# Attention scores from three passes over high and low parts of queries and keys, in place of one 32-bit product

## The chip, the cores and the metric

The kernel runs on one NeuronCore of a Trainium2 chip. The metric is the device time of one execution, in microseconds, as the median of several runs; smaller is better. The engines have short names: PE is the matrix engine (TensorE) and PEld its weight loads, ACT is ScalarE, DVE is VectorE, POOL is GpSimd, SP is SyncE, which here issues weight transfers. Each engine works through its own queue in order and waits on semaphores.

## The reference

One layer of a streaming encoder for 1024 prompt frames and 32 sample frames. It has a retention branch, a differential attention branch, a gated convolution network and a per-layer input embedding. The change touches the differential attention alone, whose core is:

```python
def diff_core(q, k, v, mask, lam):
    s = jnp.einsum('bqhmd,bkhmd->bhmqk', q, k, preferred_element_type=jnp.float32) * (DA_DK ** -0.5)
    if mask is not None:
        s = jnp.where(mask, s, jnp.finfo(jnp.float32).min)
    p = jax.nn.softmax(s, axis=-1)
    a = p[:, :, 0] - lam * p[:, :, 1]
    return jnp.einsum('bhqk,bkhe->bqhe', a.astype(v.dtype), v)
```

There are 4 heads with two maps (m = 0, 1) each, and 128 numbers per query and key. The prompt is cut into blocks of 128 queries; a block sees all keys up to its own chunk of 64. The 32 sample queries see 128 cached keys and their own 32. Queries and keys come from a projection of the normed input, are normed and rotated by position.

## The kernel before

**Number formats.** Weights and activations of the large products are kept as a high and a low part (`w_hi`, `w_lo`, `a_hi`, `a_lo`, type float32r), and a product is three PE instructions (`three`, lines 604 to 608: high by high, high by low, low by high). POOL makes the parts of a weight unit of 128x1024 (`split`, lines 497 to 506). A part lies in one of 8 slots; a unit's slot is split again when the last product that reads it is done. The attention scores are instead one plain 32-bit product per block of up to 512 keys (line 830), with the queries `q_t` as weights and the keys `k_t` as the moving operand; the trace records each as two PE instructions.

**Stages.** Gates (up to 200 us), retention (to 490 us), differential attention (490 to 1080 us), then output branches, up and down projections and the embedding.

**Order within differential attention.** All engines walk over the same steps (`for s in range(DIFF_STEPS)`), 12 steps a head. Step s projects token tile s (0 to 7 are prompt tiles of 128 rows, 8 is the 32 sample rows), and works on older tiles with a lag: `turned` is the tile one step back, `scored` two, `weighed` three, `normed` four. The three steps after a head's tiles are `fill` steps, in which PE computes six pieces of two gates from weight slots (`DIFF_GATE_SLOTS`).

PE's order in a step is: first part of the projection to queries and first key map (slots 0 to 2), scores of map 0 of the scored tile, transposes of the weighed tile's attention (line 848), rest of that projection, products with the values (line 857), scores of map 1, projection to second key map and values (slots 4 to 6), transposes of the turned tile's queries and keys into bank 4 (line 995), for tiles with over four blocks the rest of the products with the values, transposes of the normed tile (line 1011).

- Map 0's scores wait for `d_ev` of their tile: two copies on DVE (lines 1948 and 1949), the last DVE work of the step before, which wait for the transposes at line 995.
- Map 1's scores of tiles 4 to 7 wait for map 0's exponential on ACT (line 1426), as both maps use the same banks. Tiles 0 to 3 and 8 (`short`) have a bank for each map.
- ACT's order in a step is: square of the normed tile (line 1354, which waits for the transposes at line 1011 of the step before), squares of the turned tile (line 1370), roots, values (line 1390), normed tile (1399), output rows and their transfer (1411, 1414), then a table load and map 0's exponential (1426), and map 1's (1438).
- DVE's order is: maximum of map 0 (line 1871), in the first fill step the copy of the cached keys (line 1877), the copy of transposed attention that PE's line 857 waits for (line 1885), norms and rotation of the turned tile (1899, 1766 to 1774), maximum of map 1 (1914), weights of the attention (1939), the two copies.
- POOL splits a head's 8 units in this order: three for slots 0 to 2, three for slots 4 to 6, two gates.

Of the kernel before, what the change touches and what calls it, by code (L numbers as in the profile page):

```python
# [22 lines left out]
P = 128  # L23
# [40 lines left out]
EARLY = 3  # L64
PA_SLOT, PB_SLOT = 0, 4
BRIDGE_SLOT = 3
DIFF_GATE_SLOTS = (3, 7)
GATE_BANKS = (3, 2, 0, 1, 3, 2)


# [37 lines left out]
def kernel_program(nc, t):  # L108
    with ExitStack() as ctx:
        def sb(name, shape, dt=F32):  # L110
            return ctx.enter_context(nc.sbuf_tensor(name, shape, dt))
# [15 lines left out]
        a_lo = sb("a_lo", [P, KT * NT], F32R)  # L127

        a_pre = nc.alloc_sbuf_tensor_at("a_pre", [P, KT * NT], F32, offset=a_lo_at)
        full = sb("full", [P, KT * NT])  # L130
        scr = sb("scr", [P, 6 * UW])
        ident = sb("ident", [P, P])
        ones = sb("ones", [P, P])
# [100 lines left out]
        gqk = f.take(2 * P).rearrange("p (g c) -> p g c", g=2)  # L234
        mask = f.take(2 * P)
        k_t_at = f.at
        k_t = f.take(2 * (NT + PAST)).rearrange("p (m n) -> p m n", m=2)
        v_tok = f.take((TILES + 1) * DV).rearrange("p (t c) -> p t c", t=TILES + 1)
        nrm_at = f.at
        nrm = f.take(512)  # L240
        a_t = f.take(1024).rearrange("p (b n) -> p b n", b=8)
        kc = f.take(2 * P)
        rope_b = s.take(512)
        qk = s.take(2 * 512).rearrange("p (b n) -> p b n", b=2)
        e0 = s.take(1024)
        e1 = s.take(1024)
        a_w = s.take(1024)
        q_t = s.take(2 * 2 * P).rearrange("p (b m n) -> p b m n", b=2, m=2)
        o_n = s.take(2 * DV).rearrange("p (b n) -> p b n", b=2)
        o_t = s.take(2 * DV).rearrange("p (b m n) -> p b m n", b=2, m=2)  # L250
        st = s.take(48)


        at = nrm_at + 256
# [66 lines left out]
        def wait_piece(eng, h, n, pieces):  # L321

            eng.wait_ge(pieces, GATE_PIECES + 6 * h + n + 1)
# [55 lines left out]
        def score_bank(m, i):  # L379

            return 5 + m if short(i) else 5
# [114 lines left out]
        def _(pool):  # L496
            def split(before, j, slot, words=8 * P, others=0):


                landed = (before + (j - j % RAW)) * 4 + 16  # L500
                pool.wait_ge(w_landed[j % RAW], landed)
                pool.sem_inc(S["w_begun"], 1)
                raw, hi, lo = w_raw[:, j % RAW, 0:words], w_hi[:, slot, 0:words], w_lo[:, slot, 0:words]
                pool.tensor_scalar(hi, raw, 1.0, 0.0, ALU.mult, ALU.add).then_inc(S["w_hi_done"], 1)  # L504
                pool.wait_ge(S["w_hi_done"], before + (j + 1 - others))
                pool.tensor_tensor(lo, raw, hi.bitcast(F32), ALU.subtract).then_inc(S["w_split"], 1)  # L506
# [17 lines left out]
            for h in range(HEADS):  # L524
                unit = U_DIFF + (8 * h + 1 if h else 0)
                if h:
                    pool.wait_ge(S["pa_done"], h * TILES)
                    pool.wait_ge(S["a_done"], h * TILES - 1)
                else:
                    pool.wait_ge(S["ret_proj"], (HEADS - 1) * TILES)  # L530
                for j in range(3):
                    split(0, unit + j, PA_SLOT + j)
                if h == 0:
                    split(0, U_BRIDGE, BRIDGE_SLOT)
                    unit += 1
                if h:
                    pool.wait_ge(S["pb_done"], h * TILES)
                else:
                    pool.wait_ge(S["ret_proj"], HEADS * TILES)
                for j in range(3):  # L540
                    split(0, unit + 3 + j, PB_SLOT + j)
                for j in range(2):
                    if h:
                        wait_piece(pool, h - 1, 4 + j, S["gate_part"])
                    else:
                        pool.wait_ge(S["acc_done"], A_DIFF)
                    split(0, unit + 6 + j, DIFF_GATE_SLOTS[j])
            for j in range(8):
                if j == 0:
                    pool.wait_ge(S["pa_done"], HEADS * TILES)  # L550
                    pool.wait_ge(S["a_done"], HEADS * TILES - 1)
                if j in DIFF_GATE_SLOTS:
                    wait_piece(pool, HEADS - 1, 4 + (j == DIFF_GATE_SLOTS[1]), S["gate_part"])
                if j == PB_SLOT:
                    pool.wait_ge(S["pb_done"], HEADS * TILES)
                split(U_B, j, j)
            def eight_units(g):
                for j in range(8):
# [44 lines left out]
        def _(pe):  # L603
# [219 lines left out]
            def scores(m, i):  # L823

                keys, first = (P * (i + 1), 0) if i < LAST else (NS + PAST, NP)
                r = rows(i)
                for b in range(0, keys, 512):
                    n = min(512, keys - b)
                    diag = i < LAST and b + n == keys
                    last = pe.matmul(ps[0:r, score_bank(m, i) + b // 512, 0:n], q_t[:, i % 2, m, 0:r],  # L830
                                     k_t[:, m, first + b:first + b + n], start=True, stop=not diag)
                    if diag:
                        last = pe.matmul(ps[0:r, score_bank(m, i) + b // 512, n - P // 2:n], mask[:, 0:P],  # L833
                                         mask[:, P + P // 2:2 * P], start=False, stop=True)
                return last
# [340 lines left out]
        def _(act):  # L1176
# [162 lines left out]
            for s in range(DIFF_STEPS):  # L1339
# [61 lines left out]
                if stored:  # L1401
                    h, i, n = stored
                    r, b = rows(i), i % 2
                    act.wait_ge(S["dot_tr"], n + 1)
                    if n == 0:
                        act.wait_ge(ot_st[0], RET_TILES // 2 * 16)
                        act.wait_ge(ot_st[1], RET_TILES // 2 * 16)
                    if h * (5 - b) + i // 2:
                        act.wait_ge(dot_st[b], (h * (5 - b) + i // 2) * 16)
                    for m in range(2):  # L1410
                        act.activation(o_t[:, b, m, 0:r], ps[:, 7, (2 + m) * P:(2 + m) * P + r], ACT.Copy,
                                       scale=cols[:, 24 + m:25 + m]).then_inc(S["dot_ev"], 1)
                    act.wait_ge(S["dot_ev"], 2 * (n + 1))
                    act.dma_start(o_d[2 * h:2 * h + 2, :, i * P:i * P + r].rearrange("m p n -> p m n"),
                                  o_t[:, b, :, 0:r]).then_inc(dot_st[b], 16)
                if scored:
                    h, i, n = scored
                    r, b = rows(i), i % 2
                    keys = P * (i + 1) if i < LAST else NS + PAST
                    if n == 0:  # L1420
                        act.wait_ge(S["s_out"], HEADS * 32)
                        act.wait_ge(gate_st[0], (FIRST + 3) // 2 * 16)
                    act.wait_ge(S["m0_done"], n + 1)
                    if n >= 1:
                        act.wait_ge(S["a_done"], n)
                    act.activation(e0[0:r, 0:keys], score_rows(0, i), ACT.Exp, bias=st[0:r, 24 + b:25 + b],  # L1426
                                   accum_out=st[0:r, 28 + 2 * b:29 + 2 * b]).then_inc(S["e0_done"], 1)
# [6 lines left out]
                if scored:  # L1434
                    h, i, n = scored
                    r, b = rows(i), i % 2
                    act.wait_ge(S["m1_done"], n + 1)
                    act.activation(e1[0:r, 0:keys], score_rows(1, i), ACT.Exp, bias=st[0:r, 26 + b:27 + b],
                                   accum_out=st[0:r, 29 + 2 * b:30 + 2 * b]).then_inc(S["e1_done"], 1)
                fill = fill_at(s, 1)  # L1440
                if fill:
                    h, k = fill
# [214 lines left out]
        def _(dve):  # L1657
# [191 lines left out]
            for s in range(DIFF_STEPS):  # L1849
# [23 lines left out]
                now = fill_at(s, 0)  # L1873
                if now and now[1] == 0:
                    h = now[0]
                    dve.wait_ge(S["dc_tr"], h + 1)
                    dve.tensor_copy(k_t[:, :, NT:NT + PAST],
                                    ps[:, 2, 0:2 * P].rearrange("p (m n) -> p m n", m=2)).then_inc(S["dc_ev"], 1)
                if weighed:
                    h, i, n = weighed  # L1880
                    r, c = rows(i), min(4, i + 1) if i < LAST else 2
# [59 lines left out]
                if turned:  # L1941
                    h, i, n = turned
                    r, b = rows(i), i % 2
                    dve.wait_ge(S["d_tr"], n + 1)
                    if freed(i, n) > 0:
                        dve.wait_ge(S["s1_done"], freed(i, n))
                    v4 = ps[:, 4, :].rearrange("p (m n) -> p m n", m=4)
                    dve.tensor_copy(q_t[:, b, :, 0:r], v4[:, 0:2, 0:r]).then_inc(S["d_ev"], 1)
                    dve.tensor_copy(k_t[:, :, i * P:i * P + r], v4[:, 2:4, 0:r]).then_inc(S["d_ev"], 1)

            def evict(p):

# [280 lines left out]
```

## Time and profile before

| | us |
|---|---|
| median of 3 runs (lowest, highest) | 2243.19 (2242.13, 2244.16) |
| the profiled execution's own time | 2242.92 |
| its span, first to last instruction | 2241.1 |
| PE busy | 2222.3 (99%) |
| DVE, POOL, ACT busy | 1078.2, 666.0, 654.7 |

The span is what the trace shows; 1.8 us lie around it. A row of the timeline has the start from the span's start and a duration, both in us. PE's durations run past the start of the next instruction, since matmuls are pipelined; the time that one takes in a stream is the distance of the starts.

### The profile page before, as it was taken

What the parts mean: (1) busy time and instruction counts of PE and PEld (TensorE: products, weight loads), DVE (VectorE), ACT (ScalarE), POOL (GpSimd) and SP (SyncE); (2) the same over time, 40 slices, a digit from 0 to 9 for tenths busy, and PEclk for the clock granted to TensorE, in tenths of its full rate; (3) what the DMA queues carried; (4) which work ended last, traced back from release to release, by engine and by line L of the source; (5) the groups of instructions that cost most, each with busy time, mean ns of one, the idle gap of its engine ahead of it and who ended that gap; (6) DMA issues with size and microseconds to landing.
All of it is one profiled execution on the core that took longest, in us unless ns stands there. A gap on an engine that the chain in (4) does not pass through costs nothing.

```text
span 2241.1 us, 34167 instructions
## 1 busy us (share of the span) xinstructions
PE 2222.3 (99%) x13160; PEld 2091.9 (93%) x13160; DVE 1078.2 (48%) x2032; ACT 654.7 (29%) x1519; POOL 666.0 (30%) x368
## 2 busy tenths in 40 slices
PE   8999999999999999999999999999999999999999
PEld 7999777789898898998999999999999999999999
DVE  5312444445535455355145658666666663313432
ACT  5200333335535345354212222110101104334311
POOL 4522210230130400401350534223333325576520
PEclk9999999999999999999999999999999999999999
DMA  7622222230130310302851322222222126656311
GB/s 253 198 92 76 71 69 88 76 103 27 32 108 27 105 40 25 118 27 72 301 169 61 116 64 76 76 67 70 72 66 76 57 68 202 187 162 203 97 50 49
DMA packets 312666, 218.18 MB, mean 97 GB/s; under 512 B 16330, under 2 KB 303677, under 8 KB 312542
## 3 DMA queue, kind: packets, MB, share of 16 engines
q1 hardware_dynamic: 219802, 117.33, 18.1%
q10 hardware_dynamic: 92740, 99.15, 13.1%
q8 instruction: 83, 1.36, 0.3%
q14 instruction: 41, 0.34, 0.0%
HBM read 160.15 MB, written 56.29 MB: 97 GB/s over the span
## 4 chain that ended last, share of the span: by engine, by line
PE 94%; ACT 3%; DMA 1%; issue 1%; DVE 1%; ACTq 1%; DVEq 0%
PE ps L606 28%; PE ps L608 28%; PE ps L607 27%; PE ps L830 3%; PE ps L857 2%; PE ps L780 1%; PE ps L785 1%; PE ps L995 1%; PE ps L782 1%; PE ps L848 1%; ACT L1426 1%; ACT L1377 1%; DMA scr<-inv_d 0%; ACT full L1370 0%; PE ps L833 0%
## 5 line engine op out<-in xcount | busy, mean ns | idle before, releaser
L606 PE MATMUL ps<-a_hi,w_hi 128*128 128x352 f32 x2928 | 950.1, 324 | 5.3 <-DVE a_lo L1674 3.2
L608 PE MATMUL ps<-a_hi,w_lo 128*128 128x352 f32 x2928 | 940.3, 321 | 0.0
L607 PE MATMUL ps<-a_lo,w_hi 128*128 128x352 f32 x2928 | 939.5, 321 | 0.0
L504 POOL TENSOR_SCALAR w_hi<-w_raw 128x1024 fp32r<-128x1024 f32 x150 | 162.9, 1086 | 1435.8 <-PE ps L608 877.5
L606 PEld LDWEIGHTS ps<-a_hi,w_hi 128*128 128x128 f32 x2928 | 549.6, 188 | 9.3 <-issue 8.6
L607 PEld LDWEIGHTS ps<-a_lo,w_hi 128*128 128x128 f32 x2928 | 550.9, 188 | 0.4
L608 PEld LDWEIGHTS ps<-a_hi,w_lo 128*128 128x128 f32 x2928 | 550.4, 188 | 0.0
L506 POOL TENSOR_TENSOR w_lo<-w_raw,w_hi 128x1024 fp32r<-128x1024 f32 x150 | 363.5, 2423 | 12.5
L606 PE MATMUL ps<-w_hi,a_hi 128*128 128x384 f32 (+3 forms) x864 | 318.7, 369 | 0.0
L608 PE MATMUL ps<-w_hi,a_lo 128*128 128x384 f32 (+3 forms) x864 | 307.7, 356 | 0.0
L607 PE MATMUL ps<-w_lo,a_hi 128*128 128x384 f32 (+3 forms) x864 | 306.5, 355 | 0.0
L608 PEld LDWEIGHTS ps<-w_hi,a_lo 128*128 128x128 f32 (+1 forms) x864 | 154.4, 179 | 19.5
L607 PEld LDWEIGHTS ps<-w_lo,a_hi 128*128 128x128 f32 (+1 forms) x864 | 155.5, 180 | 16.8
L606 PEld LDWEIGHTS ps<-w_hi,a_hi 128*128 128x128 f32 (+1 forms) x864 | 154.9, 179 | 16.7
L581 POOL TENSOR_TENSOR w_lo<-w_raw,w_hi 128x1024 fp32r<-128x1024 f32 (+1 forms) x64 | 141.5, 2244 | 74.2 <-ACT w_hi L1571 74.2
L2052 DVE TENSOR_TENSOR scr<-ps,scr 128x704 f32<-128x704 f32 x44 | 39.2, 891 | 131.9 <-PE ps L608 131.9
L1524 ACT ACT_TABLE_LOAD x21 | 26.9, 1283 | 253.0 <-issue 253.0
L2060 DVE COPY u_last<-scr 128x4 f32 (+1 forms) x44 | 88.3, 2006 | 5.7
L1766 DVE TENSOR_TENSOR scr<-ps,full 128x128 f32<-128x128 f32 (+3 forms) x72 | 25.7, 356 | 130.0 <-ACT full L1259 128.8
L2098 DVE TENSOR_TENSOR full<-full,ps 128x352 f32 (+1 forms) x24 | 12.4, 520 | 157.0 <-PE ps L608 157.0
L1259 ACT ACTIVATE full<-ps,u_last 128x256 f32<-128x256 f32 (+1 forms) x36 | 17.0, 472 | 216.2 <-PE ps L608 208.2
L830 PE MATMUL ps<-full,scr 128*128 128x512 f32 (+4 forms) x208 | 77.3, 478 | 1.6 <-ACT scr L1426 1.3
(206 smaller groups left out, 2283.4 us busy)
## 6 DMA issues: line engine op xcount, KB each, us to landing
w_raw<-w_in SPq DMA_DIRECT2D x64, 512.0 KB, 4.2
w_raw<-w_down SPq DMA_DIRECT2D x48, 512.0 KB, 3.6
w_raw<-w_up SPq DMA_DIRECT2D x44, 512.0 KB, 3.7
hid_d<-scr ACTq DMA_DIRECT2D x22, 512.0 KB, 2.6
w_raw<-w_down SPq DMA_DIRECT2D x24, 384.0 KB, 3.2
scr<-gates_d ACTq DMA_DIRECT2D x24, 352.0 KB, 6.1
gates_d<-full ACTq DMA_DIRECT2D x13, 528.0 KB, 2.6
xt_d<-full ACTq DMA_DIRECT2D x1, 4224.0 KB
```

Of the source, the lines that this page charges most:

```text
L504: pool.tensor_scalar(hi, raw, 1.0, 0.0, ALU.mult, ALU.add).then_inc(S["w_hi_done"], 1)
L506: pool.tensor_tensor(lo, raw, hi.bitcast(F32), ALU.subtract).then_inc(S["w_split"], 1)
L581: pool.tensor_tensor(w_lo[:, slot, 0:words], w_raw[:, j % RAW, 0:words], w_hi[:, slot, 0:words].bitcast(F32), ALU.subtract).then_inc(S["w_ ...
L606: pe.matmul(out, lhs[0], rhs[0], start=start, stop=False)
L607: pe.matmul(out, lhs[0], rhs[1], start=False, stop=False)
L608: return pe.matmul(out, lhs[1], rhs[0], start=False, stop=stop)
L830: last = pe.matmul(ps[0:r, score_bank(m, i) + b // 512, 0:n], q_t[:, i % 2, m, 0:r], k_t[:, m, first + b:first + b + n], start=True, stop= ...
L857: last = pe.matmul(ps[0:r, 7, 0:DV], a_t[0:n, b, 0:r], v_tok[0:n, vt, :], start=b == 0, stop=b == every - 1)
L1524: act.activation(row(1, CW), row(1, CW), ACT.Silu).then_inc(S["silu_done"], 1)
L1766: dve.tensor_tensor(bb[:, :, 0, :], x4[:, :, 1, :], sn, ALU.mult).then_inc(prods, 1)
L2052: dve.tensor_tensor(u[:, GAP:GAP + 2 * THIRD].rearrange("p (c n) -> p c n", c=2), src[:, 0:2, :], inv[:, 0:2 * THIRD].rearrange("p (c n) - ...
L2060: dve.tensor_copy(u_last[:, bass.ds(j + half * FT, 1), :].rearrange("p a (s w) -> p (a s) w", w=GAP), ends).then_inc(S["u_last_done"], 1)
```

## The change

Queries and keys of the differential attention get a high and a low part, and each score product becomes `three`. ACT makes the high parts by copies out of PSUM, DVE the low parts by subtraction. The query buffers were two of 32-bit queries (by tile parity) and are now one of high and one of low parts, so ACT's copies wait for the tile before (`s1_done`). The low parts of the prompt keys take slot 7 of the weights (map 0 in `w_hi`, map 1 in `w_lo`); the second gate moves to slot 6, which the values' projection uses as well. The keys of sample and cache have low parts in a buffer of their own (`k_lo_last`, over the raw cached keys).

```diff
-DIFF_GATE_SLOTS = (3, 7)
+DIFF_GATE_SLOTS = (3, 6)
+KEY_SLOT = 7
...
+        k_lo = (w_hi[:, KEY_SLOT, :], w_lo[:, KEY_SLOT, :])
+
+        def key_parts(h, i):
+
+            return TILES + 9 + (TILES + 1) * h + i + 1 + (i == LAST)
...
                 for j in range(3):
+                    if h and PB_SLOT + j == DIFF_GATE_SLOTS[1]:
+                        wait_piece(pool, h - 1, 5, S["gate_part"])
                     split(0, unit + 3 + j, PB_SLOT + j)
                 for j in range(2):
-                    if h:
-                        wait_piece(pool, h - 1, 4 + j, S["gate_part"])
+                    if j:
+                        pool.wait_ge(S["pb_done"], (h + 1) * TILES)
+                    elif h:
+                        wait_piece(pool, h - 1, 4, S["gate_part"])
...
-                    last = pe.matmul(ps[0:r, score_bank(m, i) + b // 512, 0:n], q_t[:, i % 2, m, 0:r],
-                                     k_t[:, m, first + b:first + b + n], start=True, stop=not diag)
+                    high = k_hi[:, m, first + b:first + b + n]
+                    low = k_lo[m][:, b:b + n] if i < LAST else k_lo_last[:, m, :]
+                    last = three(ps[0:r, score_bank(m, i) + b // 512, 0:n], (q_hi[:, m, 0:r], q_lo[:, m, 0:r]),
+                                 (high, low), True, not diag)
...
+                cached = fill_at(s, 0)
+                if cached and cached[1] == 0:
+                    act.wait_ge(S["dc_tr"], cached[0] + 1)
+                    act.activation(k_hi[:, :, NT:NT + PAST], ps[:, 2, 0:2 * P].rearrange("p (m n) -> p m n", m=2),
+                                   ACT.Copy).then_inc(S["xs_done"], 1)
                 if scored:
...
+                if turned:
+                    h, i, n = turned
+                    r = rows(i)
+                    act.wait_ge(S["d_tr"], n + 1)
+                    if n >= 1:
+                        act.wait_ge(S["s1_done"], n)
+                    v4 = ps[:, 4, :].rearrange("p (m n) -> p m n", m=4)
+                    act.activation(q_hi[:, :, 0:r], v4[:, 0:2, 0:r], ACT.Copy)
+                    act.activation(k_hi[:, :, i * P:i * P + r], v4[:, 2:4, 0:r], ACT.Copy).then_inc(S["xs_done"], 1)
...
-                    dve.wait_ge(S["dc_tr"], h + 1)
-                    dve.tensor_copy(k_t[:, :, NT:NT + PAST],
-                                    ps[:, 2, 0:2 * P].rearrange("p (m n) -> p m n", m=2)).then_inc(S["dc_ev"], 1)
+                    dve.wait_ge(S["xs_done"], cache_parts(h))
+                    dve.tensor_tensor(k_lo_last[:, :, NS:NS + PAST], ps[:, 2, 0:2 * P].rearrange("p (m n) -> p m n", m=2),
+                                      k_hi[:, :, NT:NT + PAST].bitcast(F32), ALU.subtract).then_inc(S["dc_ev"], 1)
...
-                    dve.tensor_copy(q_t[:, b, :, 0:r], v4[:, 0:2, 0:r]).then_inc(S["d_ev"], 1)
-                    dve.tensor_copy(k_t[:, :, i * P:i * P + r], v4[:, 2:4, 0:r]).then_inc(S["d_ev"], 1)
+                    dve.tensor_tensor(q_lo[:, :, 0:r], v4[:, 0:2, 0:r], q_hi[:, :, 0:r].bitcast(F32),
+                                      ALU.subtract).then_inc(S["d_ev"], 1)
...
+                        for m in range(2):
+                            last = dve.tensor_tensor(k_lo[m][:, at], v4[:, 2 + m, :], k_hi[:, m, at].bitcast(F32),
+                                                     ALU.subtract)
...
+                    last.then_inc(S["d_ev"], 1)
```

Three places show how the queues change. First ACT, in the first fill step of a head (scored tile 7), from the output rows to the end of the step. Before:

```order
L1411 ACTIVATE scr<-ps,cols 128x128
L1414 DMA o_d<-scr 128x2x128 [waits dot_ev]
L1426 ACT_TABLE_LOAD [waits a_done]
L1426 ACTIVATE scr<-ps,scr 128x1024 [waits m0_done]
L1433 DMA new_k_sample<-scr 32x256 [waits d_rope]
L1438 ACTIVATE scr<-ps,scr 128x1024 [waits m1_done]
L1354 ACTIVATE scr<-ps 128x256 [waits dot_tr,pv_done]
```

Now (the lines are 29 to 34 further down in the changed kernel):

```order
L1440 ACTIVATE scr<-ps,cols 128x128
L1443 DMA o_d<-scr 128x2x128 [waits dot_ev]
L1448 ACTIVATE k_hi<-ps 128x2x128 [waits dc_tr]
L1460 ACT_TABLE_LOAD [waits a_done]
L1460 ACTIVATE scr<-ps,scr 128x1024 [waits m0_done]
L1467 DMA new_k_sample<-scr 32x256 [waits d_rope]
L1472 ACTIVATE scr<-ps,scr 128x1024 [waits m1_done]
L1481 ACTIVATE q_hi<-ps 128x2x32 [waits s1_done,d_tr]
L1482 ACTIVATE k_hi<-ps 128x2x32
L1383 ACTIVATE scr<-ps 128x256 [waits dot_tr,pv_done]
```

The copy of the cached keys stands between the output transfer and the exponential of map 0, and the two copies of the turned tile stand ahead of the next step's first square; in every other step of a turned tile these two are new as well.

Second DVE, at the end of the step of scored tile 6 and the start of that of tile 7. Before:

```order
L1939 SCALAR_TENSOR_TENSOR scr<-scr 128x896 [waits at1_tr,at0_tr,r_ratio]
L1948 COPY scr<-ps 128x256 [waits s1_done,d_tr]
L1949 COPY full<-ps 128x2x128
L1856 RECIPROCAL scr<-scr 128x1 [waits do_rt]
L1871 TENSOR_REDUCE scr<-ps 128x1 [waits s0_done]
L1877 COPY full<-ps 128x2x128 [waits dc_tr]
L1885 COPY full<-ps 128x512 [waits pv_done,at0_tr]
```

Now:

```order
L1982 SCALAR_TENSOR_TENSOR scr<-scr 128x896 [waits at1_tr,at0_tr,r_ratio]
L1989 TENSOR_TENSOR q_lo<-ps,q_hi 128x256 [waits xs_done]
L1994 TENSOR_TENSOR w_hi<-ps,k_hi 128x128
L1994 TENSOR_TENSOR w_lo<-ps,k_hi 128x128
L1899 RECIPROCAL scr<-scr 128x1 [waits do_rt]
L1914 TENSOR_REDUCE scr<-ps 128x1 [waits s0_done]
L1920 TENSOR_TENSOR k_lo_last<-ps,k_hi 128x2x128 [waits xs_done]
L1928 COPY full<-ps 128x512 [waits pv_done,at0_tr]
```

Two copies that waited for PE have become three subtractions that wait for ACT (`xs_done`), and so has the one for the cached keys, ahead of the copy that PE's products with the values wait for.

Third POOL, from the second unit for slots 4 to 6 to the second gate, of the second head. Before:

```order
L504 TENSOR_SCALAR w_hi<-w_raw 128x1024 [waits w_landed0]
L506 TENSOR_TENSOR w_lo<-w_raw,w_hi 128x1024 [waits w_hi_done]
L504 TENSOR_SCALAR w_hi<-w_raw 128x1024 [waits w_landed1]
L506 TENSOR_TENSOR w_lo<-w_raw,w_hi 128x1024 [waits w_hi_done]
L504 TENSOR_SCALAR w_hi<-w_raw 128x1024 [waits gate_part,w_landed2]
L506 TENSOR_TENSOR w_lo<-w_raw,w_hi 128x1024 [waits w_hi_done]
L504 TENSOR_SCALAR w_hi<-w_raw 128x1024 [waits gate_part,w_landed3]
```

Now:

```order
L525 TENSOR_SCALAR w_hi<-w_raw 128x1024 [waits w_landed0]
L527 TENSOR_TENSOR w_lo<-w_raw,w_hi 128x1024 [waits w_hi_done]
L525 TENSOR_SCALAR w_hi<-w_raw 128x1024 [waits gate_part,w_landed1]
L527 TENSOR_TENSOR w_lo<-w_raw,w_hi 128x1024 [waits w_hi_done]
L525 TENSOR_SCALAR w_hi<-w_raw 128x1024 [waits gate_part,w_landed2]
L527 TENSOR_TENSOR w_lo<-w_raw,w_hi 128x1024 [waits w_hi_done]
L525 TENSOR_SCALAR w_hi<-w_raw 128x1024 [waits pb_done,w_landed3]
```

The unit for slot 6 now waits for the last gate piece of the head before, and the second gate for the last projection into slots 4 to 6 of its own head.

## Rows read from the trace of the kernel before

**Rows 1.** The page, busy time of PE and its weight loads.
```profile
PE 2222.3 (99%) x13160; PEld 2091.9 (93%) x13160; DVE 1078.2 (48%) x2032; ACT 654.7 (29%) x1519; POOL 666.0 (30%) x368
```

**Rows 2.** All waits of PE, 485 to 1085 us: total us, times, longest.
```profile
PE ps L830 <- ACT scr L1426: 1.3, 5, 0.3
```

**Rows 3.** PE's timeline, float32r passes in a stream: start, us, instruction.
```profile
263.25 0.39 PE L606 MATMUL ps<-w_hi,a_hi 128*128 128x512 f32 x1
...
263.95 0.40 PE L606 MATMUL ps<-w_hi,a_hi 128*128 128x512 f32 x1
...
778.91 0.34 PE L606 MATMUL ps<-w_hi,a_hi 128*128 128x384 f32 x1
...
782.58 0.34 PE L606 MATMUL ps<-w_hi,a_hi 128*128 128x384 f32 x1
```

**Rows 4.** PE's timeline, map 0's scores of tiles 0 and 3, second head.
```profile
650.64 0.38 PE L830 MATMUL ps<-full,scr 128*128 128x128 f32 x2
650.86 0.33 PE L833 MATMUL ps<-full 128*128 128x64 f32 x2
...
682.90 1.02 PE L830 MATMUL ps<-full,scr 128*128 128x512 f32 x2
683.76 0.33 PE L833 MATMUL ps<-full 128*128 128x64 f32 x2
```

**Rows 5.** PE's transposes, then DVE's copies of tile 0, second head.
```profile
648.63 0.60 PE L995 MATMUL ps<-ident,scr 128*128 128x128 f32 x4
...
649.27 0.42 DVE L1948 COPY scr<-ps 128x256 f32<-128x256 f32 x1 [4.86 <-PE ps L995]
649.61 0.41 DVE L1949 COPY full<-ps 128x256 f32<-128x256 f32 x1
```

**Rows 6.** Tile 4, second head: PE, then DVE, then ACT, from its transposes on.
```profile
693.49 0.60 PE L995 MATMUL ps<-ident,scr 128*128 128x128 f32 x4
693.92 0.38 PE L1011 MATMUL ps<-ident,scr 128*128 128x128 f32 x2
695.72 1.24 PE L830 MATMUL ps<-full,scr 128*128 128x512 f32 x4
...
702.20 0.70 PE L830 MATMUL ps<-full,scr 128*128 128x512 f32 x1 [0.28 <-ACT scr L1426]
...
694.47 0.41 DVE L1949 COPY full<-ps 128x256 f32<-128x256 f32 x1
...
694.40 0.39 ACT L1354 ACTIVATE scr<-ps 128x256 f32<-128x256 f32 x1 [3.48 <-PE ps L1011]
694.68 0.20 ACT L1354 ACTIVATION_READ_ACCUMULATOR scr<-ps 128x1 f32 x1
...
701.96 0.19 ACT L1426 ACTIVATION_READ_ACCUMULATOR scr<-ps,scr 128x1 f32 x1
```

**Rows 7.** Tile 6, second head: end of map 0's exponential, start of map 1's scores.
```profile
731.54 0.19 ACT L1426 ACTIVATION_READ_ACCUMULATOR scr<-ps,scr 128x1 f32 x1
...
731.78 0.70 PE L830 MATMUL ps<-full,scr 128*128 128x512 f32 x1
```

**Rows 8.** Tile 7, second head (first fill step): ACT, DVE, PE.
```profile
745.01 1.28 ACT L1426 ACT_TABLE_LOAD   x1 [0.50 <-ACT scr L1411]
...
744.71 0.68 DVE L1885 COPY full<-ps 128x512 f32<-128x512 f32 x1
...
745.62 1.89 PE L857 MATMUL ps<-full 128*128 128x256 f32 x8
...
747.68 0.59 PE L830 MATMUL ps<-full,scr 128*128 128x512 f32 x1
```

**Rows 9.** POOL's third unit for slots 4 to 6 of the third head, PE's last gate pass.
```profile
771.62 1.05 POOL L504 TENSOR_SCALAR w_hi<-w_raw 128x1024 fp32r<-128x1024 f32 x1
772.76 2.36 POOL L506 TENSOR_TENSOR w_lo<-w_raw,w_hi 128x1024 fp32r<-128x1024 f32 x1
...
778.01 0.32 PE L608 MATMUL ps<-a_hi,w_lo 128*128 128x352 f32 x1
```

More of the change, by code:

```diff
@@ L129, in kernel_program @@
         a_pre = nc.alloc_sbuf_tensor_at("a_pre", [P, KT * NT], F32, offset=a_lo_at)
+        full_at = -(-nc.sbuf_base // 32) * 32
         full = sb("full", [P, KT * NT])
+        scr_at = -(-nc.sbuf_base // 32) * 32
         scr = sb("scr", [P, 6 * UW])
@@ L236, in kernel_program @@
         k_t_at = f.at
-        k_t = f.take(2 * (NT + PAST)).rearrange("p (m n) -> p m n", m=2)
+        f.take(2 * (NT + PAST))
         v_tok = f.take((TILES + 1) * DV).rearrange("p (t c) -> p t c", t=TILES + 1)
@@ L241, in kernel_program @@
         a_t = f.take(1024).rearrange("p (b n) -> p b n", b=8)
+        kc_at = f.at
         kc = f.take(2 * P)
+        f.take(2 * NS)
         rope_b = s.take(512)
@@ L247, in kernel_program @@
         a_w = s.take(1024)
-        q_t = s.take(2 * 2 * P).rearrange("p (b m n) -> p b m n", b=2, m=2)
+        q_at = s.at
+        s.take(2 * 2 * P)
         o_n = s.take(2 * DV).rearrange("p (b n) -> p b n", b=2)
@@ L251, in kernel_program, with cache_parts @@
         st = s.take(48)
+        q_hi, q_lo = (nc.alloc_sbuf_tensor_at(name, [P, 2, P], F32R, offset=scr_at + 4 * (q_at + n * 2 * P))
+                      for n, name in enumerate(("q_hi", "q_lo")))
+        k_hi = nc.alloc_sbuf_tensor_at("k_hi", [P, 2, NT + PAST], F32R, offset=full_at + 4 * k_t_at)
+        k_lo_last = nc.alloc_sbuf_tensor_at("k_lo_last", [P, 2, NS + PAST], F32R, offset=full_at + 4 * kc_at)
+        k_lo = (w_hi[:, KEY_SLOT, :], w_lo[:, KEY_SLOT, :])
+        def key_parts(h, i):
+            return TILES + 9 + (TILES + 1) * h + i + 1 + (i == LAST)
+        def cache_parts(h):
+            return TILES + 9 + (TILES + 1) * h + LAST + 1
         at = nrm_at + 256
@@ L555, in _ @@
                     pool.wait_ge(S["pb_done"], HEADS * TILES)
+                if j == KEY_SLOT:
+                    pool.wait_ge(S["s1_done"], HEADS * TILES)
                 split(U_B, j, j)
@@ L1943, in _ @@
                     r, b = rows(i), i % 2
-                    dve.wait_ge(S["d_tr"], n + 1)
-                    if freed(i, n) > 0:
-                        dve.wait_ge(S["s1_done"], freed(i, n))
+                    dve.wait_ge(S["xs_done"], key_parts(h, i))
                     v4 = ps[:, 4, :].rearrange("p (m n) -> p m n", m=4)
-                    dve.tensor_copy(q_t[:, b, :, 0:r], v4[:, 0:2, 0:r]).then_inc(S["d_ev"], 1)
-                    dve.tensor_copy(k_t[:, :, i * P:i * P + r], v4[:, 2:4, 0:r]).then_inc(S["d_ev"], 1)
+                    dve.tensor_tensor(q_lo[:, :, 0:r], v4[:, 0:2, 0:r], q_hi[:, :, 0:r].bitcast(F32),
+                                      ALU.subtract).then_inc(S["d_ev"], 1)
+                    at = slice(i * P, i * P + r)
+                    if i < LAST:
+                        for m in range(2):
+                            last = dve.tensor_tensor(k_lo[m][:, at], v4[:, 2 + m, :], k_hi[:, m, at].bitcast(F32),
+                                                     ALU.subtract)
+                    else:
+                        last = dve.tensor_tensor(k_lo_last[:, :, 0:NS], v4[:, 2:4, 0:r], k_hi[:, :, at].bitcast(F32),
+                                                 ALU.subtract)
+                    last.then_inc(S["d_ev"], 1)
             def evict(p):
```

## The prediction

> **What bounds the kernel now.** I read the page first: PE is busy 99% of the span [rows 1], so any time PE saves or waits shows in the total unless another chain takes over. Then PE's waits within differential attention, the only stage touched: 1.3 us in about 600, and all of them are map 1's scores waiting for map 0's exponential on ACT [rows 2]. The stage is thus bound by PE, but in some tiles ACT is right behind. The timelines of single tiles show where.
>
> In tile 4 the wait is 0.28 us [rows 6]. Followed back, ACT has run without a break of its own making since the square at line 1354, which the dot transposes of the step before released (693.92 + 0.38 = 694.30, start 694.40). It ends the exponential at 701.96 + 0.19 = 702.15, and PE starts at 702.20. Here the step is as long as ACT's chain. In tile 6 the exponential ends at 731.73 and PE starts at 731.78 with no idle time: the same hop of 0.05 us, so ACT and PE arrive together [rows 7]. Tile 5 lies between and is taken like tile 4. In tiles 0 to 3, 7 and 8 PE alone sets the pace.
>
> The third view is the hand-over to the scores. In tile 0 the transposes end at 648.63 + 0.60 = 649.23, DVE's copies run from 649.27 to 649.61 + 0.41 = 650.02 [rows 5], and scores start at 650.64 [rows 4]: 0.62 us of slack. In tile 4 the copies end at 694.88 and scores start at 695.72: 0.84 us [rows 6]. Tiles 1 and 2 are like 0, 3 and 5 like 4; later ones have more.
>
> **PE's passes.** A 32-bit product of 512 columns takes 683.76 - 682.90 = 0.86 us, one of 128 columns 0.22 us [rows 4]; that is a line of 1.67 ns a column, so 256, 384 and 160 columns take 0.43, 0.65 and 0.27 us. A float32r pass of 512 columns takes (263.95 - 263.25) / 3 = 0.233 us, one of 384 takes (782.58 - 778.91) / 21 = 0.175 us [rows 3]. Three passes of 512 are 0.70 (0.16 less than now), of 384 0.525 (0.12 less); on the line through both, 256 costs 0.35 (0.08 less) and 160 0.22 (0.05 less).
>
> No float32r pass of fewer than 352 columns is in the trace. For 128 columns the line gives 0.058 a pass. The upper bound is that a narrow pass takes as long as the whole 32-bit product, 0.22. I take 0.108, from the four transposes of 128 columns with weights of their own, (693.92 - 693.49) / 4 [rows 6], the nearest instruction of that width with one record: three passes are then 0.324, 0.10 more than now. For 160 columns of 32 queries I keep the line; its upper bound is 0.27 a pass.
>
> On weight loads there is a rule against this change: the Trainium skill, TensorE: Matmul & The Clock Gate, section LDWEIGHTS, puts a load at columns / 1.2, so 107 ns for 128 columns however few columns then stream past. [...] By that rule the total would be what I forecast; by the line alone 1.9 us less.
>
> Per head and map there are six products of 512, two each of 384, 256 and 128, one of 160. For both maps: 12 x 0.16 + 4 x 0.12 + 4 x 0.08 + 2 x 0.05 - 4 x 0.10 = 2.4 us less a head, 9.7 us in four heads. That is what the change brings on PE if nothing waits.
>
> **The hand-over grows.** Until now it was two copies on DVE, 0.75 us. Now ACT does two copies of 128x256 out of PSUM, then DVE three subtractions. For ACT I take the square of that shape at line 1354: 0.39 us long, the next instruction 0.28 after its start [rows 6], so both end 0.67 after the first starts. Then a hop of 0.04 (649.23 to 649.27) and DVE: 0.34 from the first start to the second [rows 5], and two halves, which I put at 0.19 and 0.26 by their columns, 0.79 in all. The path is 0.67 + 0.04 + 0.79 - 0.75 = 0.75 us longer. PE's release costs 0.05, and a weight load that isn't ahead 0.11 more (a first pass of 0.70 in place of 0.59 [rows 6, 8]). So PE waits 0.75 + 0.16 - 0.62 = 0.29 us in tiles 0, 1 and 2, and 0.07 in 3; in 4 and 5 the same 0.07 vanishes within the longer wait that follows; from 6 on nothing.
>
> **ACT's chain starts later.** The copies stand ahead of the next step's square. In tile 4 they start at 694.09 + 0.04 and hold ACT for 2 x 0.28, until 694.69, where it began at 694.40 before: 0.29 us. Map 1's scores of tiles 4 and 5 start that much later, since ACT ends last there, and what PE saves in map 0 is lost in waiting. In tile 6 and 7 PE multiplies with the values between the two groups of transposes, at least 0.43 us (a 32-bit product of 256 columns), so ACT isn't later; but in tile 6 map 0's gain is lost too, as ACT is not earlier either.
>
> **The first fill step.** DVE's copy of the cached keys needed only PE. Its subtraction needs ACT's copy, which is queued behind the output transfer and so starts at 745.01, where the table load stands now [rows 8]. It ends 0.39 later, DVE starts at 745.44, its next instruction 0.34 later; that is the copy of the transposed attention (0.68), queued behind. It ends at 746.46, where it ended at 745.39. PE's products with the values start at 746.62, not 745.62: 1.00 us late, and map 1's scores with them. The exponential moves by 0.28 only, so it doesn't add.
>
> **POOL.** The third unit for slots 4 to 6 is now split after the last gate pass: 778.01 + 0.32 = 778.33, plus a unit's 772.76 + 2.36 - 771.62 = 3.50, makes 781.83 [rows 9]. PE wants it at 782.58, where that projection's first pass stands [rows 3]. The 0.75 us left cover the two hops; cost nothing. The second gate's unit is split after the last projection into slots 4 to 6, and PE wants it a whole step later: a unit's 3.50 us are hidden. ACT's squares of tiles 1 and 2 come later as well, behind the copies; in tile 4 ACT goes from the square to the end of the exponential in 7.75 us [rows 6], and the rotation that PE's next transposes need doesn't wait for all of it, so within a step of over 10 us I let it cost nothing.
>
> **The sum, by tile, for one head** (passes of both maps, then waits): tile 0: +0.20 + 0.29 = +0.49; tile 1: -0.16 + 0.29 = +0.13; tile 2: -0.24 + 0.29 = +0.05; tile 3: -0.32 + 0.07 = -0.25. Tile 4: ACT +0.29, map 1's passes -0.06: +0.23. Tile 5: +0.29 - 0.24 = +0.05. Tile 6: map 1 alone, -0.28. Tile 7: +1.00 - 0.32 = +0.68. Tile 8: -0.10. Together +1.0 us a head, +4.0 in four: 2242.9 + 4.0 = 2246.9 for an execution like the profiled one, which was 0.3 under the median; so 2247.2 against the median of 2243.2. The gain of 9.7 us goes into waits of 13.7.
>
> With 128 columns at 0.058 a pass tile 0 and map 1 of tile 4 lose 0.45 us a head: 2245.4. With the upper bounds (0.22 and 0.27 a pass) tile 0 adds 0.67, tile 4's map 1 0.34, tile 8 1.2: 2.2 us a head, 8.8 in all, 2256.0.
>
> **Rivals.** *Narrow passes are dear* (30%): 128 and 160 columns cost a pass what the whole 32-bit product costs. For it: nothing narrow in this format is in the trace. Against: between 384 and 512 columns the time falls with the columns. 2256, slower; it decides as soon as a pass of 128 exceeds about 0.13 us.
>
> *The waits stay covered* (17%), the faster side: ACT's and DVE's parts are quicker than the rows of their shape, or PE's recorded starts run ahead of its columns, so that the added path fits in the slack; it decides where the path grows by under 0.46 us (0.62 - 0.16). Then 0.29 in three tiles, 0.07 and twice 0.29 go, 1.5 us a head, 6 in all: 2241; and with the fill step's 1.0 covered too, 2237. For it: ACT and DVE are idle when the transposes end [rows 5, 6]. Against: the copies' price is a row of the same shape from the same source, and ACT is already last in tile 4.
>
> *POOL is late at a head's start* (8%): the hops and the split exceed 4.25 us. If POOL falls back by a whole unit, three heads wait 2.75 us each: 2255.
>
> **Chances.** A change under 0.2%, 4.5 us, can't be told from none. My forecast has 45%: it lies just inside, with 0.25 of that within, 0.18 slower, 0.02 faster. Narrow passes and POOL are slower, 38%. Covered waits are half faster, half the same. Faster 0.11, same 0.33, slower 0.56. The range goes from 2238 to 2258: the lower end takes in most of the covered waits, the upper the dear narrow passes.
>
> **What would show it.** Right: map 0's scores of tiles 0 to 2 wait about 0.3 us for DVE; map 1's of tiles 4 and 5 wait some 0.5 to 0.7 for ACT, tile 6's about 0.3; line 857 of tile 7 waits over 1 us for DVE's copy; passes of 512 stand 0.233 apart; PE's busy time falls by some 10 us while its idle time in the stage grows from 1.3 to about 15. Wrong: passes of 128 at 0.2 us or 0.06; ACT's copies well off 0.39; a wait of PE for POOL where a head begins; or PE idle for under 5 us.

## The result, and the profile after

The changed kernel takes 2248.43 us (median of 10 runs, 2247.25 to 2250.03) beside 2243.51 us of the kernel before on the same chip (10 runs, 2241.98 to 2248.78): a ratio of 1.0021, 95% interval [1.0012, 1.0029]. It is 4.9 us slower, between 2.7 and 6.5 by the interval; the forecast was 4.0.

First, the page's busy line after, which answers to [rows 1]:

```profile
PE 2218.4 (99%) x13264; PEld 2104.7 (94%) x13264; DVE 1078.2 (48%) x2064; ACT 675.5 (30%) x1595; POOL 666.4 (30%) x368
```

PE has 104 more instructions (three records in place of two, in 104 products), is still busy 99% of the span, and its busy time fell by 3.9 us. Where does the stage stretch? The first and last start of the turned tile's transposes bound it (the two times ahead of the semicolon), before and then after:

```profile
L995 PE MATMUL ps<-ident,scr x144: 221/272/273, 501.4 to 1047.7; 128*128 128x128 f32 x128, 32*128 32x32 f32 x16
```

```profile
L1024 PE MATMUL ps<-ident,scr x144: 221/272/275, 502.8 to 1053.1; 128*128 128x128 f32 x128, 32*128 32x32 f32 x16
```

Before, 546.3 us lie between them, after, 550.3: 4.0 us more. The last tile's scores come behind the last start and give 0.5 us back, so the stage costs 3.5 us. (That it starts 1.4 us later is no part of the change: the code ahead is the same, and over this case's profiled kernels that start scatters from 501.4 to 503.6.)

Now PE's waits in the stage, beside [rows 2]; below them the one wait that shows on the weight loads alone:

```profile
PE ps L633 <- ACT scr L1460: 5.0, 12, 0.6
PE ps L886 <- DVE full L1928: 4.1, 4, 1.0
```

```profile
PEld ps L633 <- DVE w_lo L1994: 4.2, 12, 0.3
```

PE's own list grew from 1.3 us in 5 waits to 9.1 us in 16 (a third line of the answer, 0.8 us at the window's start, belongs to the stage before): map 1's scores behind ACT's exponential (12 times: tiles 4 to 6), and the products with the values behind DVE's copy once a head (tile 7). The 4.2 us in 12 waits of the weight loads come on top: map 0's scores of tiles 0 to 2 behind DVE's low parts. These are missing from PE's own list because PE's recorded passes run on to the end of their pipeline and cover the gap. They aren't lost in full either: these scores start some 0.19 us later than before, 2.2 us in 12 tiles. Such covered gaps would also explain why PE's busy time fell by 3.9 us and not by the 10 that were forecast for the passes; no run shows that by itself.

The timeline of tile 0 in the second head (start, duration, engine) answers to [rows 4, 5]:

```profile
650.69 0.60 PE L1024 MATMUL ps<-ident,scr 128*128 128x128 f32 x4
...
651.32 0.38 ACT L1481 ACTIVATE q_hi<-ps 128x256 fp32r<-128x256 f32 x1 [7.24 <-PE ps L1024]
...
651.60 0.38 ACT L1482 ACTIVATE k_hi<-ps 128x256 fp32r<-128x256 f32 x1
...
652.01 0.42 DVE L1989 TENSOR_TENSOR q_lo<-ps,q_hi 128x256 fp32r<-128x256 f32 x1 [5.54 <-ACT k_hi L1482]
...
652.55 0.28 DVE L1994 TENSOR_TENSOR w_lo<-ps,k_hi 128x128 fp32r<-128x128 f32 x1
...
652.89 0.33 PE L633 MATMUL ps<-k_hi,q_hi 128*128 128x128 f32 x1
...
653.05 0.28 PE L634 MATMUL ps<-w_hi,q_hi 128*128 128x128 f32 x1
...
653.16 0.28 PE L635 MATMUL ps<-k_hi,q_lo 128*128 128x128 f32 x1
...
653.28 0.38 PE L862 MATMUL ps<-full 128*128 128x64 f32 x2
```

The hand-over runs as priced: ACT's second copy starts 0.28 behind the first, DVE 0.03 behind its end, and the low parts end at 652.55 + 0.28 = 652.83, which is 2.14 after the transposes start, where the copies before ended 1.39 after (650.02 - 648.63). PE starts at once. A pass of 128 columns takes 0.11 us (653.05, 653.16, 653.28).

Tile 4 of the second head, beside [rows 6]:

```profile
696.32 0.60 PE L1024 MATMUL ps<-ident,scr 128*128 128x128 f32 x4
...
696.95 0.38 ACT L1481 ACTIVATE q_hi<-ps 128x256 fp32r<-128x256 f32 x1 [2.98 <-PE ps L1024]
...
697.50 0.39 ACT L1383 ACTIVATE scr<-ps 128x256 f32<-128x256 f32 x1
...
705.33 0.19 ACT L1460 ACTIVATION_READ_ACCUMULATOR scr<-ps,scr 128x1 f32 x1
...
705.58 0.50 PE L633 MATMUL ps<-k_hi,q_hi 128*128 128x512 f32 x1 [0.62 <-ACT scr L1460]
```

ACT's square stood 0.91 behind the transposes (694.40 - 693.49), now 697.50 - 696.32 = 1.18, with the two copies ahead of it. The exponential ended 8.66 us behind the transposes (702.15 - 693.49) and now ends 9.20 behind them (705.52 - 696.32), and PE waits 0.62 us, where it waited 0.28. Half of those 0.54 us is the two copies. The other half is in this head alone, where ACT stands idle 0.27 us longer within the chain (0.69 us ahead of its line 1428, 0.42 in the other heads); there tile 4 waits 0.51 or 0.52. What lengthens that idle time isn't shown.

Tile 7, the first fill step, beside [rows 8]:

```profile
748.06 0.38 ACT L1448 ACTIVATE k_hi<-ps 128x256 fp32r<-128x256 f32 x1 [0.46 <-ACT scr L1440]
...
748.47 0.42 DVE L1920 TENSOR_TENSOR k_lo_last<-ps,k_hi 128x256 fp32r<-128x256 f32 x1 [1.25 <-ACT k_hi L1448]
748.81 0.68 DVE L1928 COPY full<-ps 128x512 f32<-128x512 f32 x1
...
749.55 1.99 PE L886 MATMUL ps<-full 128*128 128x256 f32 x8 [1.02 <-DVE full L1928]
...
750.76 0.19 ACT L1460 ACTIVATION_READ_ACCUMULATOR scr<-ps,scr 128x1 f32 x1
...
751.63 0.48 PE L633 MATMUL ps<-k_hi,q_hi 128*128 128x512 f32 x1
```

DVE's subtraction waits for ACT's copy of the cached keys, the copy of the transposed attention is queued behind it, and PE waits 1.02 us for that. By then the exponential is done (750.95), so map 1 doesn't wait for it.

### The profile page after: what moved, and what is told of

It is laid out like the page before. It is cut to its first block, busy times and chain, and to the rows that moved or that the text cites. A ratio compares the mean times of both kernels' runs of the same rounds, so it can differ in the third digit from the quotient of the medians.

```text
span 2245.4 us, 34484 instructions
## 1 busy us (share of the span) xinstructions
PE 2218.4 (99%) x13264; PEld 2104.7 (94%) x13264; DVE 1078.2 (48%) x2064; ACT 675.5 (30%) x1595; POOL 666.4 (30%) x368
## 4 chain that ended last, share of the span: by engine, by line
PE 91%; ACT 5%; DMA 1%; issue 1%; DVE 1%; ACTq 1%; DVEq 0%
PE ps L633 28%; PE ps L635 28%; PE ps L634 28%; PE ps L886 2%; ACT L1406 1%; ACT full L1399 1%; PE ps L807 1%; PE ps L1024 1%; PE ps L812 1%; ACT L1460 1%; PE ps L809 1%; ACT scr L1460 1%; ACT scr L1440 0%; DMA scr<-inv_d 0%; DMA gates_d<-scr 0%
## 5 line engine op out<-in xcount | busy, mean ns | idle before, releaser
L525 POOL TENSOR_SCALAR w_hi<-w_raw 128x1024 fp32r<-128x1024 f32 x150 | 162.7, 1085 | 1440.0 <-PE ps L635 1304.1
L886 PE MATMUL ps<-full 128*128 128x256 f32 (+2 forms) x304 | 76.1, 384 | 4.5 <-DVE full L1928 4.1
```

The costliest lines, as they stand in the source:

```text
L886: last = pe.matmul(ps[0:r, 7, 0:DV], a_t[0:n, b, 0:r], v_tok[0:n, vt, :], start=b == 0, stop=b == every - 1)
```

## The experiments

All were run beside the kernel before, whose median over these comparisons was 2243.9 to 2244.1 us. The theory: the passes save about what was forecast, and three waits (tile 7's DVE queue, ACT's later chain, the hand-over) take more than that back. The main rivals: the passes themselves are slow, or POOL with one slot less. A difference from the changed kernel's 2248.43 us is one between two comparisons, in which the kernel before itself took 2243.5 and 2243.9 us, so a few tenths of it mean nothing. The distances between a tile's transposes and the next tile's are firmer: nearly all agree over the four heads within some 0.05 us, but for ACT's 0.27 us above.

**The cached keys' low parts behind the copy that PE waits for.** In DVE's step:

```diff
-                now = fill_at(s, 0)
-                if now and now[1] == 0:
-                    ...  # wait for ACT, k_lo_last = cached keys - k_hi
                 if weighed:
                     ...  # a_t copy, at0_ev
+                now = fill_at(s, 0)
+                if now and now[1] == 0:
+                    ...  # the same, moved
```

> The changed kernel with one edit: in the first fill step DVE makes the low parts of the cached keys behind the copy of the transposed attention, not ahead of it. Theory (the gain on PE goes into waits for ACT and DVE): the wait of 1.0 us of PE's value products for that copy goes in all four heads; but ACT's copy of the cached keys still delays map 0's exponential, which then ends last at some 10.2 us after tile 7's transposes, so map 1's scores come 0.6 us earlier a head and not 1.0. 2.5 us faster than the changed kernel, about 2246. Rival (the loss is spread over PE's passes or is the weight slot's): no difference, 2248.4.

Measured: 2245.57 us (2243.80 to 2247.59), ratio 1.0008 [0.9999, 1.0017], 2.9 us under the changed kernel's median. PE's timeline of tile 7:

```profile
748.71 1.89 PE L886 MATMUL ps<-full 128*128 128x256 f32 x8
...
751.37 0.50 PE L633 MATMUL ps<-k_hi,q_hi 128*128 128x512 f32 x1 [0.44 <-ACT scr L1460]
```

The values no longer wait. DVE's subtraction still does (0.66 us, for ACT's copy), now at no one's cost. But the step gets only 0.6 of the 1.02 us back: map 1's scores now wait 0.44 us for the exponential, which ACT's copy of the cached keys still delays. One wait uncovered the next.

**The turned tile's high parts by DVE, not ACT.** ACT's two copies go; DVE makes them just ahead of its subtractions, so the hand-over stays as long as it was and only ACT's chain is relieved:

```diff
-                    act.activation(q_hi[:, :, 0:r], v4[:, 0:2, 0:r], ACT.Copy)
-                    act.activation(k_hi[:, :, i * P:i * P + r], v4[:, 2:4, 0:r], ACT.Copy).then_inc(S["xs_done"], 1)
...
+                    dve.tensor_copy(q_hi[:, :, 0:r], v4[:, 0:2, 0:r]).then_inc(S["sc_done"], 1)
+                    dve.tensor_copy(k_hi[:, :, at], v4[:, 2:4, 0:r]).then_inc(S["sc_done"], 1)
...
```

> The changed kernel with the high parts of the turned tile's queries and keys made by DVE (two copies, then the three subtractions), so that ACT has none of it; the cached keys as in the changed kernel. Theory: the hand-over is as long as before, so tiles 0 to 2 still wait 0.1 to 0.2 us, but ACT's chain starts 0.29 us earlier in tiles 3, 4 and 5, and map 1's scores with it: 0.9 to 1.0 us a head, 3.5 to 4.2 us in all, about 2244.5. Rival (the tiles' waits come from the longer hand-over, whichever engine works on it): no difference within 0.7 us, 2248.

Measured: 2244.43 us (2242.69 to 2247.32), ratio 1.0004 [0.9994, 1.0013]: 4.0 us less. PE's waits in the stage:

```profile
PE ps L886 <- DVE full L1919: 4.1, 4, 1.0
PE ps L633 <- ACT scr L1460: 3.2, 12, 0.5
```

The waits for ACT fall from 5.0 to 3.2 us; tile 4 is back at 0.28. By the distances from tile to tile, tiles 4 and 5 give back 2.3 us in four heads, tile 3, where the forecast saw no wait for ACT, 1.1 (next section), tiles 0 to 2 some 0.6; the first head's tile 6 loses 0.2. The hand-over itself stays. Its first two instructions on DVE in tile 0, and PE's scores:

```profile
650.49 0.43 DVE L1983 CAST q_hi<-ps 128x256 fp32r<-128x256 f32 x1 [4.85 <-PE ps L1024]
650.83 0.41 DVE L1984 CAST k_hi<-ps 128x256 fp32r<-128x256 f32 x1
```

```profile
652.03 0.33 PE L633 MATMUL ps<-k_hi,q_hi 128*128 128x128 f32 x1
```

The transposes start at 649.85 in this kernel, so scores start 2.18 us after them instead of 2.20: five instructions on one engine take as long as two and three on two engines with a hop between. So no run shortened the hand-over, and its price is read from the rows of tiles 0 to 2 alone.

**Both, and the cached keys' high parts by DVE too.**

```diff
-                    act.activation(k_hi[:, :, NT:NT + PAST], ..., ACT.Copy).then_inc(S["xs_done"], 1)
...
+                    dve.tensor_copy(k_hi[:, :, NT:NT + PAST], cached).then_inc(S["sm_done"], 1)
...
```

> All high parts by DVE, those of the cached keys too, and these behind the copy of the transposed attention: both edits, and ACT as free as in the kernel before. Theory: the gains add, 0.95 us in tiles 3 to 5 and 1.0 in tile 7 of each head: 8 us less than the changed kernel, about 2240.5, which is 3 us less than the kernel before; the rest of the gain on PE stays lost where ACT's chain sets the pace (tiles 4 to 6). Rival (the passes themselves gain nothing): not under 2243.5.

Measured: 2240.63 us (2238.57 to 2242.06), ratio 0.9983 [0.9974, 0.9992]: 7.8 us under the changed kernel and 3.3 under the kernel before (1.8 to 5.8 by the interval), so it beats both. PE's waits, then the busy line:

```profile
PE ps L633 <- ACT scr L1455: 3.3, 12, 0.5
```

```profile
PE 2218.5 (99%) x13264; PEld 2106.7 (94%) x13264; DVE 1102.9 (49%) x2140; ACT 655.2 (29%) x1519; POOL 666.7 (30%) x368
```

PE has the changed kernel's passes; what went are 5.8 of the 9.1 us of waits in its list, tile 7's whole 4.1 among them. ACT is back at the 655 us it had before the change, and DVE carries 25 us more at no cost.

**Two passes instead of three.** Leaves out low queries by high keys, so the scores lack that part:

```diff
-                    last = three(ps[0:r, ...], (q_hi[:, m, 0:r], q_lo[:, m, 0:r]), (high, low), True, not diag)
+                    out = ps[0:r, score_bank(m, i) + b // 512, 0:n]
+                    pe.matmul(out, q_hi[:, m, 0:r], high, start=True, stop=False)
+                    last = pe.matmul(out, q_hi[:, m, 0:r], low, start=False, stop=not diag)
```

> The changed kernel without the third pass of the scores (the low part of the queries by the high part of the keys is left out of the computation; all parts are still made). It takes 4.55 us of PE's passes out of each head, 18.2 in all (six of 0.232, two each of 0.175, 0.118 and 0.112, one of 0.075 for each map). Theory: in tiles 4, 5 and 6 what map 0's scores save is waited for ACT again (0.34, 0.35 and 0.41 us), in tile 7 for DVE's late copy (0.46), in tile 3 for ACT's output rows (0.23): 1.8 us a head lost, so 11 us less than the changed kernel, about 2237.5. Rival (PE is the bound all over the stage, as its 99% say): the full 18 us, 2230.

Measured: 2237.36 us (2235.82 to 2239.60), ratio 0.9970 [0.9960, 0.9981]. The pass left out is, a head, 12 times 0.233 us (512 columns), 4 times 0.175 (384), 4 times 0.118 (256, as measured after), 4 times 0.11 (128) and twice 0.07 (160): 4.55 us, 18 in four heads. 11 came off. PE's waits:

```profile
PE ps L860 <- ACT scr L1461: 7.3, 12, 0.6
PE ps L887 <- DVE full L1929: 5.9, 4, 1.5
PE ps L887 <- ACT scr L1441: 1.6, 5, 0.3
```

The waits listed grow from 9.1 us to 14.8; those of tiles 0 to 2 for DVE, on the weight loads, stay at 4.2. In tiles 3 to 7 what map 0's scores save is waited for again, as ACT's and DVE's chains end last there; what map 1's scores save counts.

**The slot alone.** The kernel before with 32-bit scores, the second gate in slot 6, and slot 7 empty:

```diff
-DIFF_GATE_SLOTS = (3, 7)
+DIFF_GATE_SLOTS = (3, 6)
...
+                    if h and PB_SLOT + j == DIFF_GATE_SLOTS[1]:
+                        wait_piece(pool, h - 1, 5, S["gate_part"])
...
```

> This is the kernel before with only the weight slots changed: one slot given over, the gate and projection units splitting into the slots left, and 32-bit scores as before. Theory: POOL's split has 0.75 us in hand at a head's start (see the prediction), so the slot costs nothing and all that the change moved lies in the three passes and the copies they need: 2243 to 2245 us, within 0.1% of the kernel before, no PE wait for POOL in differential attention, and PE's waits there still about 1.3 us, all for ACT. Rival: the slot was the price, and POOL's units come late behind PE at heads 1 to 3; then the time is that of the changed kernel, 2247 to 2249 us or more, with waits of PE for POOL's w_hi or w_lo of 1 us or more a head.

Measured: 2243.87 us (2242.65 to 2245.25), ratio 0.9998 [0.9989, 1.0007]. PE's waits in the stage, beside [rows 2]:

```profile
PE ps L837 <- ACT scr L1433: 1.4, 5, 0.3
```

The slot costs nothing that can be measured, and PE never waits for POOL.

## Why the prediction was right, point by point

The cost per tile is read as the distance from a tile's transposes to the next tile's, after less before. The starts are those of the second head; those of the third head's first tile, which close tile 8, are 795.58 and 798.78.

| tile | start before | start after | predicted us | measured us |
|---|---|---|---|---|
| 0 | 648.63 | 650.69 | +0.49 | +0.46 |
| 1 | 658.40 | 660.92 | +0.13 | +0.12 |
| 2 | 669.07 | 671.71 | +0.05 | +0.13 |
| 3 | 680.68 | 683.45 | -0.25 | +0.06 |
| 4 | 693.49 | 696.32 | +0.23 | +0.49 (other heads +0.18) |
| 5 | 707.80 | 711.12 | +0.05 | +0.07 |
| 6 | 722.42 | 725.81 | -0.28 | -0.30 (first head -0.53) |
| 7 | 737.71 | 740.80 | +0.68 | +0.64 |
| 8 | 753.53 | 757.26 | -0.10 | -0.53 |

The two odd heads are ACT's idle time of some 0.27 us again: it fell into tile 4 of the second head after the change, and into tile 6 of the first head before it.

*Passes.* 0.233 us for 512 columns and 0.108 for 128 were taken. In tile 0 a pass of 128 takes 0.11 (653.05 to 653.16). In tile 4's map 1 these rows show one of 512, then the first two of 128:

```profile
706.15 0.39 PE L635 MATMUL ps<-k_hi,q_lo 128*128 128x512 f32 x1
706.38 0.22 PE L633 MATMUL ps<-k_hi,q_hi 128*128 128x128 f32 x1
706.44 0.28 PE L634 MATMUL ps<-w_lo,q_hi 128*128 128x128 f32 x1
```

The pass of 512 takes 0.23. The first of 128 takes 0.06, what the prediction's line gives, and only the next takes 0.11 (the third starts at 706.55). So three passes of 128 take 0.28 us behind a wide pass, 0.04 less than was taken. The rival "narrow passes are dear", which began at 0.13, falls. (By the prediction's own times the line alone gives 2245.4, which is 1.8 us under 2247.2 and not 1.9.)

*Hand-over.* The path ends 2.14 us after the transposes start, as summed. Scores of tiles 0 to 2 start some 0.19 us later behind their transposes (in tile 0 2.20 for 2.01), not 0.29: the load that isn't ahead costs within the first pass (0.16 us from 652.89 to 653.05, where the next takes 0.11) and not ahead of it. In these three tiles the sums agree but for 0.08 in tile 2. That goes where DVE makes the high parts (+0.07 in that run); why it was there isn't shown.

*ACT's chain, tiles 4 to 6.* Right in place and size: 0.5 to 0.6 us of wait in tiles 4 and 5. In tile 6 map 0's gain is lost too, with a listed wait of 0.18: map 1's scores start 9.36 us behind the transposes before (731.78 - 722.42) and after (735.17 - 725.81):

```profile
734.92 0.19 ACT L1460 ACTIVATION_READ_ACCUMULATOR scr<-ps,scr 128x1 f32 x1
...
735.17 0.50 PE L633 MATMUL ps<-k_hi,q_hi 128*128 128x512 f32 x1 [0.18 <-ACT scr L1460]
```

Taking the copies off ACT brought tiles 4 and 5 of this head to -0.05 and -0.19, where the passes alone were summed at -0.06 and -0.24, so the cause is shown.

*The fill step.* 1.00 predicted, 1.02 measured; moving the subtraction took it away. "So it doesn't add", said of the exponential, held only while the larger wait stood: without it 0.44 us of it appears.

*POOL.* No wait for POOL after the change, and none with the slot alone: right.

*Signs.* One sign of being right was not met: PE's busy time fell by 3.9 us and not by some 10, and the idle time in its list grew to 9.1 and not to about 15.

Two steps were wrong. They erred in opposite directions, by 0.3 and 0.4 us a head, and that they nearly cancelled in the total is luck.

*Tile 3*, -0.25 predicted, +0.06 measured. The prediction followed ACT's later chain only to the exponential of tiles 4 to 6. But ACT's output rows of the step are in the chain too, and PE's products with the values wait for them. Before, then after:

```profile
686.04 0.62 ACT L1411 ACTIVATE scr<-ps,cols 128x128 f32<-128x128 f32 x2
...
686.71 0.34 PE L608 MATMUL ps<-w_hi,a_lo 128*128 128x384 f32 x1
...
686.89 1.46 PE L857 MATMUL ps<-full 128*128 128x256 f32 x6
```

```profile
689.08 0.62 ACT L1440 ACTIVATE scr<-ps,cols 128x128 f32<-128x128 f32 x2
...
689.42 0.34 PE L635 MATMUL ps<-w_hi,a_lo 128*128 128x384 f32 x1
...
689.85 1.32 PE L886 MATMUL ps<-full 128*128 128x256 f32 x5
```

Before, PE's products follow the pass by 0.18, its usual distance, 0.23 behind ACT's end (686.66). After, ACT ends at 689.70 and PE, which could go on at 689.60, starts at 689.85. PE hadn't waited before, so no list of waits showed this neighbour; its slack was under 0.1 us. With two passes, where PE comes earlier still, the list does name it: 1.6 us behind ACT's line 1441, four of the five waits in tile 3. With ACT relieved, the tile is near its price:

```profile
688.43 0.34 PE L635 MATMUL ps<-w_hi,a_lo 128*128 128x384 f32 x1
688.64 1.53 PE L886 MATMUL ps<-full 128*128 128x256 f32 x6
```

These are the rows of the kernel whose turned high parts are made by DVE: 0.21 us between the two, and the tile is 0.18 us shorter than in the kernel before (0.18 to 0.23 over the heads).

*Tile 8*, -0.10 predicted, -0.53 measured. The 32-bit product of 160 columns was put on the line through 128 and 512, 0.27 us, though its own row stood in the trace. Before, then after:

```profile
755.29 0.38 PE L1011 MATMUL ps<-ident,scr 128*128 128x128 f32 x2
755.60 0.46 PE L830 MATMUL ps<-full,scr 128*32 128x160 f32 x2
755.99 0.65 PE L848 MATMUL ps<-ident,scr 128*128 128x128 f32 x4
```

```profile
759.02 0.38 PE L1040 MATMUL ps<-ident,scr 128*128 128x128 f32 x2
...
759.16 0.32 PE L633 MATMUL ps<-k_hi,q_hi 128*32 128x160 f32 x1
...
759.32 0.24 PE L634 MATMUL ps<-k_lo_last,q_hi 128*32 128x160 f32 x1
...
759.39 0.24 PE L635 MATMUL ps<-k_hi,q_lo 128*32 128x160 f32 x1
...
759.47 0.60 PE L877 MATMUL ps<-ident,scr 128*128 128x128 f32 x4
```

The product took 0.39 us (755.60 to 755.99), three passes take 0.31. And it started 0.31 us behind the two transposes, the passes start 0.14 behind: 0.25 us less in all, for each of two maps.

The measured tiles sum to 3.5 us over the four heads, the prediction to 4.0; the chip's interval, 2.7 to 6.5, holds both and doesn't tell them apart. No row accounts for the 1.4 us between 3.5 and the medians' 4.9, which are within it.

## What to carry to other kernels

On an engine that is busy 99% of the time, a gain of its own is real only in the steps where no other chain ends close behind: before adding an instruction to a neighbour's queue, look up every instruction behind it that the busy engine waits for, those with zero wait and little slack too. Put new work on the engine with slack at that place, and behind the instruction that is being waited for: here the same passes were 4.9 us slower or 3.3 us faster than plain 32-bit products by that alone, the engine and the place of the copies. And price an instruction from its own row where there is one, not from a line through others.

## What the runs showed of the hardware

In a row of narrow float32r passes with weights of 128 queries the weight loads set the pace, not the columns. 160 columns past the weights of 32 queries take 0.07 us (759.32 to 759.39), 128 columns past those of 128 queries 0.11 us (653.05 to 653.16), though they are fewer. The Trainium skill, TensorE: Matmul & The Clock Gate, section LDWEIGHTS, puts a load at columns / 1.2 in ns, by which the estimate is 27 ns for 32 weights and 107 for 128; the trace agrees, since only the second exceeds the time that the passes' own columns need on the line of the wider ones (0.073 and 0.058). The first narrow pass behind a wide one is the exception: with the same weights and columns it takes 0.06 us (706.38 to 706.44), and behind it the weight loads start 0.11 apart (706.38, 706.49, 706.60).

A 32-bit product with 32 queries as weights stood apart from its neighbours by more than its columns ask: 0.39 us for 160 columns, where 128 queries with 128 columns take 0.22 [rows 4]. Why was not tried.

DVE's copies of 128x256 out of PSUM into float32r start 0.34 us apart (650.49 to 650.83), ACT's 0.28 (651.32 to 651.60); what DVE loses there it saves on the hop between the engines.
